# Where the split of the first FFN weight chunk stands against the last o^T eviction, and the order of eight output products

## The reference, cut to what matters

```python
o = attention(...)                     # (256, 1024)
x = layer_norm(ALPHA * x + o @ w_o)    # output products, then LayerNorm
up, gate = split(x @ w_in, 2)          # FFN, 22 tiles of 128 hidden features
x = layer_norm(ALPHA * x + (gelu(conv3(up)) * gate) @ w_out)
```

## Time and profile before

| | |
|---|---|
| median of 3 runs | 638.14 us (637.22 to 638.71) |
| the profiled execution's own time | 634.84 us |
| its span, first to last instruction | 633.0 us |
| mean granted TensorE clock | 0.997 |
| busy: TensorE, VectorE, ScalarE, GpSimd | 613.4, 447.4, 335.8, 63.9 us |
| HBM traffic | 108.23 MB read, 1.05 MB written |

### The profile page before, as it was taken

One profiled execution on the slowest core, in us unless ns is written; L12 is line 12 of the kernel. 1 busy time (PEld: TensorE's weight loads), 2 busy tenths in 40 slices (PEclk: granted clock), 3 DMA queues, 4 the chain that ended last, 5 costly groups with the idle time before them and its releaser, 6 DMA issues. The chain is left out here.

```text
span 633.0 us, 9437 instructions
## 1 busy us (share of the span) xinstructions
PE 613.4 (97%) x3317; PEld 507.1 (80%) x3317; DVE 447.4 (71%) x800; ACT 335.8 (53%) x550; POOL 63.9 (10%) x85
## 2 busy tenths in 40 slices
PE   8999999999999999999889999989999999999995
PEld 6777777798888888889768788768988888888894
DVE  5657477577777777777786676668776777777786
ACT  5667567446444444456326785863545544455450
POOL 4400000420000000000340020044000000000002
PEclk9999999999999999999999999999999999999998
DMA  8973334444555555555368434443634555555521
GB/s 291 338 249 134 134 133 135 134 134 133 200 199 199 199 199 183 174 177 183 146 203 302 160 134 133 134 134 121 211 110 168 188 183 174 176 196 199 199 67 68
DMA packets 68682, 109.67 MB, mean 173 GB/s; under 512 B 2044, under 2 KB 47404, under 8 KB 68140
## 3 DMA queue, kind: packets, MB, share of 16 engines
q1 hardware_dynamic: 68012, 105.09, 49.0%
q0 software_dynamic: 640, 4.20, 1.7%
HBM read 108.23 MB, written 1.05 MB: 173 GB/s over the span
## 5 line engine op out<-in xcount | busy, mean ns | idle before, releaser
L798 DVE TENSOR_TENSOR w_lo<-raw,w_hi 128x2048 fp32r<-128x2048 f32 (+1 forms) x115 | 206.0, 1804 | 68.8 <-ACT w_hi L594 68.8
L594 ACT ACTIVATE w_hi<-raw 128x2048 fp32r<-128x2048 f32 (+1 forms) x125 | 182.0, 1495 | 37.7 <-PE wide L1087 37.7
L1270 PE MATMUL score<-xT,w_hi 128*128 128x512 f32 x288 | 103.2, 401 | 1.5 <-DVE w_lo L798 1.1
L1085 PE MATMUL wide<-w_hi,xT 128*128 128x512 f32 (+1 forms) x256 | 98.4, 384 | 1.9 <-DVE w_lo L856 0.8
L1087 PE MATMUL wide<-w_hi,xT 128*128 128x512 f32 (+1 forms) x256 | 93.4, 365 | 0.0
L1086 PE MATMUL wide<-w_lo,xT 128*128 128x512 f32 (+1 forms) x256 | 93.0, 363 | 0.0
L1272 PE MATMUL score<-xT,w_lo 128*128 128x256 f32 x288 | 80.5, 280 | 0.0
L733 ACT ACTIVATE conv<-up_sum,conv_cols 128x256 f32<-128x256 f32 x36 | 21.7, 602 | 97.1 <-DVE up_sum L997 97.1
L1270 PEld LDWEIGHTS score<-xT,w_hi 128*128 128x128 f32 x288 | 54.0, 188 | 19.2 <-issue 7.2
L1085 PE MATMUL wide<-w_hi,hT_hi 128*128 128x512 f32 x176 | 68.8, 391 | 0.0
L1087 PE MATMUL wide<-w_hi,hT_lo 128*128 128x512 f32 x176 | 68.7, 390 | 0.0
(11 more groups left out here) (181 smaller groups left out, 992.1 us busy)
## 6 DMA issues: line engine op xcount, KB each, us to landing
raw<-in_ffn_w_in SPq DMA_DIRECT2D x44, 1024.0 KB, 5.1
raw<-in_ffn_w_out SPq DMA_DIRECT2D x22, 1024.0 KB, 4.9
raw<-in_a_w_qkv SPq DMA_DIRECT2D x9, 1024.0 KB, 7.0
raw<-in_w_kv_shared SPq DMA_DIRECT2D x8, 1024.0 KB, 5.1
raw<-in_a_w_o SPq DMA_DIRECT2D x4, 1024.0 KB, 4.8
raw<-in_b_w_q SPq DMA_DIRECT2D x4, 1024.0 KB, 5.0
raw<-in_b_w_o SPq DMA_DIRECT2D x4, 1024.0 KB, 4.9
raw<-in_a_w_qkv SPq DMA_DIRECT2D x6, 512.0 KB, 8.7
```

The source lines that it names most:

```text
L594: ins = nc.scalar.activation(w_hi[slot][:, part], raw[slot][:, part], ACT.Copy)
L798: ins = nc.vector.tensor_tensor(w_lo[slot][:, part], raw[slot][:, part], w_hi[slot][:, part].bitcast(F32), ALU.subtract)
L1085: nc.tensor.matmul(dst, a_hi, b_hi, start=start, stop=False, skip_group_check=True)
L1270: nc.tensor.matmul(parts, w_hi[slot][:, cols], xT[:, :, kt, :], start=kt == 0, stop=False, skip_group_check=True)
```

## The change

The order of eight products, the needs of one chunk's high split, and the steps that the scheduler knows:

```diff
-    products += [("wo", kt, 0, half) for half in range(2) for kt in range(4, 8)]
+    products += [("wo", kt, 0, half) for pair in ((4, 5), (6, 7)) for half in range(2) for kt in pair]
...
         for half in range(2):
-            after[("split_hi", c, half)], after[("split_lo", c, half)] = [], [("split_hi", c, 1)]
+            after[("split_hi", c, half)] = []
+            if c < first_chunk + 16:
+                after[("split_lo", c, half)] = [("split_hi", c, 1)]
...
+    for c in range(first_chunk + 16, first_chunk + 18):
+        if ("split_hi", c, 0) in after:
+            after[("split_hi", c, 0)].append(("out_hi", 7))
```

## The result

The changed kernel takes 642.19 us (median of 6 runs, 641.15 to 642.76) against 638.42 us for the kernel before in the same comparison (6 runs, 636.27 to 639.41). The ratio is 1.0088, interval 1.0064 to 1.0111: slower, clear of the noise. Run once more beside the last experiment it took 641.01 us against 635.86, ratio 1.0082 (1.0055 to 1.0109). The profiled execution took 641.76 us, span 639.9 against 633.0, mean granted clock 0.989 against 0.997.

A forecast was written before the change was run, and what follows sets the result against it. TensorE was taken as the bound, busy 613.4 of 633.0 us, so only its waits matter. Layer 1's loss of 4.03 plus layer 0's 0.11 gave 4.1 us slower, 638.14 to 642.3 us, range 637.9 to 645.5.

The forecast's parts named there:

- The order: Both layers: derived sequence of instructions, with outT 7 after (5,0,1), and split 65 behind out_hi 7 on ScalarE.
- Layer 1, TensorE: End of attention, layer 1: out_hi 7 at 424.55, (7,0,0) at 425.60, last first-token product 1.88 us earlier.
- The full 1.9 us of gain: Layer 1, TensorE: at most 1.9 us gained by earlier outT 7 and three following products instead of five.
- Layer 1, GpSimd: Layer 1 LayerNorm: later split 65 delays L838, and split 66 begins ahead of L847 and blocks it.
- the loss of 4.03: Layer 1: second L847 done at 438.50 instead of 434.47 because it takes turns with GpSimd's split of chunk 66.
- rival (a): Layer 1: first L847 gets through, only the second waits for one half split; loss 2.03, 640.3 us; chance 0.17.
- the 0.55 us that were to come back: Layer 1: second tokens' LayerNorm regains 0.55 us, off TensorE's path.
- Layer 0: Layer 0 LayerNorm after attention: L838 ends 0.11 us later behind GpSimd's split; no collision at L847.
- The case I called likeliest: Whole kernel: 4.03 + 0.11 = 4.1 us slower, 642.3 us, no clock loss; chance 0.52 including (e)'s different order, 641.9.
- (b): Layer 1: the forecast collision plus TensorE's clock falling after its pauses, 2.5 us more, 644.8 us; chance 0.11.
- The upper bound of 4.4 us: Layer 1, in (b): most that a slow TensorE pace could cost over the next 7 us.
- nothing here scales: Whole kernel: the 4.1 us loss is added unscaled to the 638.14 median, giving 642.3.

The follow-up runs named there:

- the last experiment: e7: e4 plus GpSimd's low splits after std_inv held behind both L847 at layer 0's last LayerNorm; 631.58 us against 635.86 before, ratio 0.9934.
- e4: Changed kernel with the high splits of chunks 16 and 65 held behind out_hi 6 instead of out_hi 7; 633.80 us, ratio 0.9959 to the kernel before.
- e5: Changed kernel plus 14 and 7 dummy matmuls keeping TensorE busy in layer 1's two pauses before the transposes; 638.80 us against 636.12 before, ratio 1.0049.
- e6: Changed kernel with GpSimd's low split of chunk 66 in four pieces of 128x512 instead of two of 128x1024; 640.00 us against 636.12 before, ratio 1.0067.
- e1: Kernel before with only the order of the eight products changed (pairs of k tiles), no hold on the split; 634.79 us against 636.52, ratio 0.9967.
- e3: Changed kernel with GpSimd's low split of chunk 66 waiting until both L847 of the first tokens are done; 636.42 us, ratio 1.0001 to before.
- e2: Changed kernel with the old product order, so only the high splits of chunks 16 and 65 are held behind out_hi 7; 635.79 us, ratio 0.9986 to before.
- e7: e4 plus GpSimd's low splits after std_inv held behind both L847 at layer 0's last LayerNorm; 631.58 us against 635.86 before, ratio 0.9934.
- e8: The changed kernel run again, unaltered, beside e7 and the kernel before; 641.01 us against 635.86, ratio 1.0082.

## Why the prediction was right

**The order** came out as derived, on all engines of both layers. **Layer 1, TensorE**: `out_hi` 7 was put at 424.55 and stands at 424.81 less 0.28, 424.53; (7,0,0) at 425.60, and 425.86 less 0.28 is 425.58; the residuals were to be 1.37 apart, and 426.86 to 428.23 is 1.37. The full 1.9 us of gain exist: e4 shows them as 1.90. **Layer 1, GpSimd**: L838 was put at 3.2 and L847 at 5.5 us, measured 3.24 and 5.46; the loss of 4.03 is 4.02 in e5. GpSimd's second split was ahead of L847 by 0.26 or 0.27 us, where 0.23 were forecast, in both profiles of the changed kernel, in e5 and in e6; rival (a) never came. The second tokens' L838, 1.95 before and 1.40 now, is the 0.55 us that were to come back off TensorE's path. The reading that carried it all was the pair of L847 that already collided in the kernel before: it gave the price of a collision. That the two engines take turns was read from one `std_inv` between two L838; with several instructions waiting on both sides it was a forecast, which the changed kernel (5.46 us) and e6 (3.31 us) bear out. The rule of the Trainium skill in "SBUF — State Buffer", section "SBUF: two separate sides", is an exclusive lock for the whole instruction. The traces agree with it: 5.46 us beside splits of 128x1024, 3.31 beside splits of 128x512 in e6. **Layer 0**: 0.11 was forecast; the shift grows from 0.11 to 0.23 there (L847 at 123.89 against 123.66), so 0.12.

**What was off.** The case I called likeliest left the clock alone, and (b), the same with the clock falling, had a chance of 0.11. It is (b) that happened: all six runs of the first comparison had a mean clock of 0.986 to 0.989. Its price was right (2.5 put down, 2.37 measured), its chance was not: a pause of 3.76 us and one of 1.64 with little work between them is more than anything in the trace before. The prediction leaned on a longest pause of 1.72 us that cost no clock; the whole trace before has one of 1.96 (at 316.14), also without a fall, and neither is evidence about one of 4. (The upper bound of 4.4 us in (b) is 4.3 by its own figures, 7 x (629/390 - 1).) By the spans, (b) is also the sum that holds: 6.9 us measured, 4.1 + 2.5 = 6.6 forecast.

That the median of 642.2 nevertheless met 642.3 is luck: a second error, in the opposite direction, nearly cancelled the first. I added the change to 638.14, with the words that nothing here scales. The kernel before has no fixed time: of 56 further runs 17 lie between 634.2 and 634.5 us, all with a mean clock of 0.996 or 0.997, and the others up to 641.2, the slowest with 0.987. The profiled execution, at 634.84, was near the undisturbed time, and the base for the sum, not 3.3 us under it. 634.84 + 6.6 = 641.4; measured were 642.2 and 641.0. So two steps of the working were off: the clock left alone, and how the profiled execution stands to the median. Part of the second stays open: the medians differ by 3.8 and 5.2 us, where the spans of the changed kernel's two profiles lie 6.9 and 6.3 above that of the kernel before, and nothing here shows why the changed kernel's median lies only 1.1 us above its lowest time (641.01, 639.87) and that of the kernel before 1.5 (635.86, 634.34). Lowest times agree with the traces better, but only to within about 1 us: +5.7 for the changed kernel (6.39 in layer 1), -1.3 for e1 (-1.36), -2.1 for e4 (-1.90), +4.2 for e5 (4.02), but +0.7 for e3 (-0.15) and +4.9 for e6 (3.82).

## What to carry to other kernels

When two engines that can block each other have an order only because one of them gets its input late, making everything before it earlier can turn that order round: look for the operation whose start was safe by time and not by a wait (here GpSimd's split of chunk 66, whose input came 0.1 us behind the end of the last L847), and either fix its order by a semaphore or leave the slack. Test both parts of a change alone: here each one was harmless or a gain (-1.36 and -0.51 us), and together they cost 6.4. And fill a wait with work of its own length: the hold on `out_hi` 6 puts 2.0 us of splitting into 1.8 us of waiting, where the hold on 7 put it on the critical path of the next stage.

## What the runs showed of the hardware that was not expected

The clock falls after shorter pauses than I had allowed for, but not always. In the profiled execution of e4 it fell twice at the end of layer 0, after pauses of 1.96 and 1.83 us, and in those of the kernel before and the changed kernel it did not, though their pauses there are the same (1.96 and 1.82 us in the kernel before). The timeline of PE of e4:

```profile
316.22 0.66 PE L1103 MATMUL score<-ident,xs 128*128 128x128 f32 x4 [1.96 <-DVE xs L852]
...
318.12 0.63 PE L1091 MATMUL wide<-w_lo,hT_hi 128*128 128x512 f32 x1
...
329.88 0.66 PE L1103 MATMUL turn<-ident,xs 128*128 128x128 f32 x4 [1.83 <-DVE xs L852]
...
332.22 0.63 PE L1092 MATMUL wide<-w_hi,xT 128*128 128x512 f32 x1
```

The granted clock was 0.63 from 316 to 320 us and 0.59 from 330 to 334, against 1.00 in both stretches of the changed kernel. In e4 the first transposes behind the pause of 1.96 us are still fast (0.66 us); in e2, behind the same pause, they are already slow (1.07). What decides in which executions the clock falls, and when, stays open. That it is what spreads the times of all these kernels is argued and not shown, since no run removed both pauses: five traces have a lowered clock there (e1, e2, e3, e4 and e6), five have not (before, changed, e5, e7 and e8).
